# A state-space scan rewritten for sub-chunks of four steps, in a three-block model on one core

## The reference

```python
mag = jnp.exp(lam_re * dt); ang = lam_im * dt          # transition lambda = mag * e^(i ang)
bb_re = q_re[..., None] * br - q_im[..., None] * bi     # q depends on lambda
bu_re = jnp.einsum('blgc,gnc->blgn', u32, bb_re)        # and bu_im
_, _, s_re, s_im = lax.associative_scan(_scan_combine, (a_re_t, a_im_t, bu_re, bu_im), axis=1)
y = (jnp.einsum('blgn,gcn->blgc', s_re, c_re) - jnp.einsum('blgn,gcn->blgc', s_im, c_im) + d_skip * u32)
g = jax.nn.gelu(y); hg = g @ w_glu
out = hg[..., :1024] * jax.nn.sigmoid(hg[..., 1024:])
```

## Time and profile before

| | |
|---|---|
| median of 3 runs | 3033.09 us (3031.11 to 3035.19) |
| profiled execution | 3031.87 us, span 3030.1 us |
| mean granted TensorE clock | 0.99 |
| TensorE, VectorE, ScalarE, GpSimd busy | 97%, 57%, 47%, 2% of the span |
| weights and inputs read | 511.58 MB, 170 GB/s over the span |
| s_in stage, first granule to first of glu | 2468 to 2756 us |

### The profile page before, as it was taken

How to read it: one execution, slowest core, us unless ns; L and a number is a source line. 1 busy time by engine, 2 the same in 40 slices (tenths; PEclk the granted TensorE clock), 3 DMA queues, 4 the chain that set the end, 5 groups by cost and what they waited for, 6 DMA issues and landing times.

```text
span 3030.1 us, 34851 instructions
## 1 busy us (share of the span) xinstructions
PE 2924.2 (97%) x13709; PEld 2403.3 (79%) x13709; DVE 1731.7 (57%) x2222; ACT 1415.6 (47%) x1809; POOL 74.0 (2%) x66
## 2 busy tenths in 40 slices
PE   8999999999999999999999999999999999989998
PEld 7888877788888888878887788888888877556876
DVE  5875655644544454554445545544454569998545
ACT  5543375544444444454446444444444454444444
POOL 0000000000000000000000000000000002210000
PEclk9999999999999999999999999999999999999999
DMA  6532245565555555555552565555655554335443
GB/s 236 176 126 93 89 140 189 179 194 193 181 194 194 194 185 190 193 177 185 188 187 86 175 207 187 190 191 194 194 190 185 194 175 132 98 104 168 172 157 125
DMA packets 255293, 515.45 MB, mean 170 GB/s; under 512 B 8240, under 2 KB 8464, under 8 KB 254144
## 3 DMA queue, kind: packets, MB, share of 16 engines
q1 hardware_dynamic: 252896, 501.61, 50.0%
q0 software_dynamic: 2272, 12.10, 1.2%
HBM read 511.58 MB, written 2.10 MB: 170 GB/s over the span
## 4 chain that ended last, share of the span: by engine, by line
PE 87%; DVE 9%; ACT 2%; issue 2%; DMA 0%; SPq 0%; DVEq 0%; ACTq 0%
PE acc L462 80%; PE side L658 2%; DVE u L1609 2%; DVE u L2210 1%; DVE pc L1609 1%; ACT ar L1009 1%; DVE wlo L1621 1%; DVE ar L1609 1%; PE side L524 1%; PE side L769 1%; PE side L553 1%; DVE ar L1612 0%; ACT whi L1020 0%; DMA raw<-in_ev_w_in 0%; ACT L1009 0%
## 5 line engine op out<-in xcount | busy, mean ns | idle before, releaser
L1621 DVE TENSOR_TENSOR wlo<-raw,whi 128x1024 fp32r<-128x1024 f32 x948 | 1155.3, 1226 | 1114.3 <-ACT whi L1020 1113.5
L1020 ACT ACTIVATE whi<-raw 128x1024 fp32r<-128x1024 f32 x948 | 996.8, 1059 | 1201.3 <-PE acc L462 1199.7
L462 PE MATMUL acc<-whi,xh 128*128 128x512 f32 x3072 | 841.1, 396 | 10.9 <-ACT whi L1020 4.7
L462 PE MATMUL acc<-wlo,xh 128*128 128x512 f32 x3072 | 825.4, 391 | 22.6 <-DVE wlo L1621 22.6
L462 PE MATMUL acc<-whi,xl 128*128 128x512 f32 x3072 | 824.1, 390 | 0.0
L462 PEld LDWEIGHTS acc<-wlo,xh 128*128 128x128 f32 x3072 | 577.6, 188 | 146.7 <-DVE wlo L1621 26.0
L462 PEld LDWEIGHTS acc<-whi,xl 128*128 128x128 f32 x3072 | 578.5, 188 | 122.2
L462 PEld LDWEIGHTS acc<-whi,xh 128*128 128x128 f32 x3072 | 568.9, 189 | 132.7 <-issue 9.6
L462 PE MATMUL acc<-whi,hTh 128*128 128x512 f32 x720 | 194.2, 392 | 2.7 <-ACT u L1009 2.7
L462 PE MATMUL acc<-wlo,hTh 128*128 128x512 f32 x720 | 193.3, 391 | 0.0
L462 PE MATMUL acc<-whi,hTl 128*128 128x512 f32 x720 | 193.3, 390 | 0.0
(11 more groups left out here) (227 smaller groups left out, 1356.5 us busy)
## 6 DMA issues: line engine op xcount, KB each, us to landing
raw<-in_ffn_w_gate SPq DMA_DIRECT2D x88, 1024.0 KB, 5.1
raw<-in_ffn_w_up SPq DMA_DIRECT2D x88, 1024.0 KB, 5.1
raw<-in_ffn_w_down SPq DMA_DIRECT2D x88, 1024.0 KB, 5.0
raw<-in_ev_w_in SPq DMA_DIRECT2D x56, 1024.0 KB, 5.1
raw<-in_od_w_in SPq DMA_DIRECT2D x48, 1024.0 KB, 5.1
raw<-in_w_in SPq DMA_DIRECT2D x32, 1024.0 KB, 5.3
raw<-in_ev_w_out SPq DMA_DIRECT2D x16, 1024.0 KB, 5.0
raw<-in_od_w_out SPq DMA_DIRECT2D x16, 1024.0 KB, 5.0
```

Source lines behind the costliest of these rows:

```text
L462: mm = pe.matmul(acc[2 * pair + t][:], x[:, k0 + j, t * P:t * P + P], w[:, ring, j], start=start and j == 0, stop=stop and j == 1)
L1020: act.activation(whi[:, place % RING], raw_granule(place), ACT.Copy).then_inc(S("hi_done"), 1)
L1621: dve.tensor_tensor(wlo[:, place % RING], raw_granule(place), whi[:, place % RING].bitcast(F32), ALU.subtract).then_inc(S("lo_done"), 1)
```

## The change

The scan works on sub-chunks of four steps (`SUB = 4`). Per group, 4 steps x 16 channels make 64 rows. Four matrices are made from the parameters: `b_lhs` maps the 64 inputs of a sub-chunk to its contribution to the 64 complex states (B times lambda to the power 3 to 0), `c_lhs` maps the state at the end of the sub-chunk before to the 64 outputs (C times lambda to the power 1 to 4), and `t_lhs` maps the inputs to the outputs within a sub-chunk, the skip term included. The recurrence then has 64 steps instead of 256, with lambda to the fourth. Two groups share a 128-partition tile, one on the partitions 0 to 63 and one on 64 to 127, so nearly all its matmuls have 64 rows, 64 weight columns and 64 (or 16) moving columns, in pairs on the two halves (`half(g)`).

What moves or is new, by engine:

- GpSimd: no table arguments any more. The parameters are loaded during the feed-forward layer ahead; 16 transfers of 32 partitions x 512 elements move the projected inputs (`step_pj`) from one place of on-chip memory to another (`xs`), so that sub-chunks lie on partitions. The pooling weights, the last gain row and `p` are loaded later than before.
- TensorE: `turn_b`, `kernel_base`, `kernel_shift`, `turn_u`, `inputs`, `outputs`, `back_steps`, `back_features` in s_in in place of `turn_wide`, `ssm_in`, `ssm_out` and two of four turns; `parameter_columns` and `turn_c` in dn1b.
- VectorE: `angles`, `factors` and `input_matrix` in dn1b; `expand_b` six times, `expand_c` eight times, `table_args` four times, one `rotate` with eight scans of 64 elements and one `unrotate` per channel tile. The gelu result's low part comes from `gate_lo`.
- ScalarE: evacuations of the above, gelu four times on 512 columns instead of eight times on 256, two tables at a time.

The diff, cut to its core:

```diff
-SSM_AT = [22 + 5 * ct for ct in range(8)]
+SUB = 4
+STEPS = TOK // SUB
+V_AT = [17, 23, 28, 34, 39, 43, 47, 51]
+Y_AT = [23, 28, 34, 40, 45, 49, 53, 56]
+BACK_AT = [55, 57, 59, 61]
@@ gpsimd
-            for ct in range(8):
-                pool.tensor_tensor(angle, iota, f, ALU.mult).then_inc(S("tab_arg"), 1)
...
+            for q in range(2):
+                pool.wait_ge(S("projected"), 2 * (PROJ0["s_in"] + q) + 2)
+                for t in range(TT):
+                    for k in range(SUB):
+                        pool.dma_start(xs[64 * q + 32 * t:64 * q + 32 * t + 32, k], step_pj[k:P:SUB, t])\
+                            .then_inc(S("x_moved"), 16)
@@ tensor
+            def turn_c(m):
+                pe.wait_ge(S("bc_in"), 64)
+                b = claim(side[3 - m], "c_turned", m + 1)
+                for ct in range(8):
+                    for g in range(2):
+                        mm = pe.matmul(b[half(g), 64 * ct:64 * ct + 64], c_raw[:, m, ct], pick[:, g],
+                                       start=True, stop=True)
-            def ssm_in(n):
-                for m in range(2):
-                    mm = pe.matmul(b[:, m * TOK:m * TOK + TOK], bt[rows, m, ct], uT[rows, ct], start=True, stop=True)
+            def turn_b(q, f):
+                for r in range(4):
+                    for m in range(2):
+                        for g in range(2):
+                            if g:
+                                mm = pe.matmul(b[half(g), o:o + 64], x, one, start=True, stop=True)
+                            else:
+                                pe.transpose(b[half(g), o:o + 64], x, one)
+            def kernel_base(q):
+                for a in range(16):
+                    for m in range(2):
+                        for g in range(2):
+                            mm = pe.matmul(b[half(g), 16 * a:16 * a + 16], b_exp(q)[half(g), a, m],
+                                           c_bar[half(g), m, 16 * q + a], start=(m == 0), stop=(m == 1))
+            def turn_u(e, bank):
+                pe.wait_ge(S("x_spread"), e + 1)
+                for r in range(8):
+                    mm = pe.transpose(b[:, 64 * r:64 * r + 64], x, ident[half(q), half(q)])
+            def inputs(ct):
+                for r in range(4):
+                    for m in range(2):
+                        for g in range(2):
+                            mm = pe.matmul(b[half(g), o:o + 64], b_lhs[half(g), 4 * ct + r, m], ug[half(g), 4 * ct + r],
+                                           start=True, stop=True)
+            def outputs(ct):
+                for r in range(4):
+                    for g in range(2):
+                        pe.matmul(b[half(g), o:o + 64], t_lhs[half(g), a].rearrange("p t c -> p (t c)"), ug[half(g), a],
+                                  start=True, stop=False)
+                    for m in range(2):
+                        for g in range(2):
+                            mm = pe.matmul(b[half(g), o + 1:o + 64], c_lhs[half(g), a, m], z[half(g), r, m, 0:63],
+                                           start=False, stop=(m == 1))
@@ scalar
+            def x_spread(q):
+                act.wait_ge(S("x_moved"), 128 * (q + 1))
+                for k in range(2):
+                    run(xw[half(q), a], xs.rearrange("p t (a c) -> p a t c", c=16)[half(q), a], ACT.Copy, "x_spread")
@@ vector
+            def expand_b(q, d, n):
+                times_lam(b_bar, d, q)
+                tt(b_exp(q)[:, :, 0, o], by_part(work1)[:, 0], by_part(work2)[:, 1], sub, "expanded")
+                tt(b_exp(q)[:, :, 1, o], by_part(work1)[:, 1], by_part(work2)[:, 0], add, "expanded")
+            def rotate(ct):
+                tt(a, v, cos.unsqueeze(2).to_broadcast([P, 4, 2, STEPS]), mult, "rotated")
+                tt(b[:, :, 0], v[:, :, 1], sin, mult, "rotated")
+                tt(b[:, :, 1], v[:, :, 0], sin, mult, "rotated")
+                tt(z[:, :, 0], a[:, :, 0], b[:, :, 0], add, "rotated")
+                tt(z[:, :, 1], a[:, :, 1], b[:, :, 1], sub, "rotated")
+                for k in range(4):
+                    for m in range(2):
+                        done(dve.tensor_tensor_scan(z[:, k, m], decay, z[:, k, m], 0.0, mult, add))
```

More of the change, by code:

```diff
@@ L539, in features_use, with turn @@
                 return use
-            def turn(name, c):
+            def turn(name, c, halves=(0, 1), bank=None):
                 pe.wait_ge(S("projected"), 2 * (PROJ0[name] + c) + 2)
                 pj = pj_at(name)
-                for j in range(2):
+                for j in halves:
                     n = 2 * TURN[name, c] + j
@@ new lines, in s_aside @@
+                if at_ == 25:
+                    turn_u(3, side[3])
+                if at_ in (26, 28, 30, 32):
+                    turn_b(1, (26, 28, 30, 32).index(at_))
+                if at_ == 27:
+                    kernel_base(1)
+                if at_ == 32:
+                    turn("s_in", 2)
+                if at_ == 35:
+                    b = claim(side[2], "t_done", 5)
+                    kernel_shift(1, 1, b)
+                    kernel_shift(1, 2, b)
+                if at_ == 39:
+                    kernel_shift(1, 3, claim(side[2], "t_done", 6))
@@ new lines, in s_aside @@
+                if at_ == 45:
+                    turn("s_in", 3, (0,), 3)
+                if at_ == 48:
+                    turn("s_in", 3, (1,), 3)
+                for ct in range(8):
+                    if at_ == V_AT[ct]:
+                        inputs(ct)
+                    if at_ == Y_AT[ct]:
+                        outputs(ct)
+                if at_ in BACK_AT:
+                    back_steps(BACK_AT.index(at_))
+                if at_ in (58, 60, 62):
+                    back_features((58, 60, 62).index(at_), side[2])
@@ new lines, in back_out, with gate_hi @@
+            def back_out(e):
+                if e >= 2:
+                    act.wait_ge(S("back2"), e - 1)
+                for k in range(2):
+                    act.wait_ge(S("back1"), 2 * e + k + 1)
+                    q = half(0)
+                    run(at(BACK, 4, CH)[q, 2 * (e % 2) + k].rearrange("p (t a c) -> p a t c", t=SUB, a=8),
+                        side[k][q, :].rearrange("p (a t c) -> p a t c", a=8, t=SUB), ACT.Copy, "back_done")
+            def gate_hi(e, bank):
+                act.wait_ge(S("back2"), e + 1)
+                run(gate_h[:, 2 * e:2 * e + 2].rearrange("p k (j t) -> p k t j", t=SUB),
+                    bank[:].rearrange("p (k t j) -> p k t j", k=2, t=SUB), ACT.Copy, "gh_done")
@@ new lines, in s_aside @@
+                if at_ == 41:
+                    t_out(1, 3, side[2])
+                if at_ == 42:
+                    tables(3)
+                if at_ in (47, 50):
+                    k = (47, 50).index(at_)
+                    act.wait_ge(S("turned"), 2 * TURN["s_in", 3] + k + 1)
+                    run(turned_to("s_in", 3, k), side[3][:].rearrange("p (a b) -> p a b", a=2), ACT.Copy, "turn_done")
+                if at_ in (31, 43, 52, 59):
+                    gelu((31, 43, 52, 59).index(at_))
@@ L2336, in glu_out @@
                            at(SGS, TT, 1024)[:, t, CH * m:CH * m + CH], ALU.mult, "mixed")
[L2338 to L2342 removed]
             def glu_aside(c, j):
+                if (c, j) == (0, 0):
+                    gate_lo(2, side[2])
+                if (c, j) == (0, 1):
+                    gate_lo(3, side[3])
                 for k, where in enumerate(POOL_AT):
```

831 lines of the change are left out of this document (477 added, 354 removed).

## The result

The change makes the kernel faster: 3014.19 us in the median of four runs (3012.33 to 3014.44) against 3034.08 (3031.11 to 3035.19), a ratio of 0.9937, 95% interval 0.9925 to 0.9948. That is 20 us less; forecast were 39 us less. The time lies inside the range of 2970 to 3024, but nearly on the value of a rival (3016) whose mechanism did not happen: that it came near is luck. The profiled execution took 3012.33 us, with a span of 3010.6 us.

What follows compares the result with a forecast made beforehand. VectorE was taken to bound s_in; after, TensorE needs 174.1 + 2.7 start + 60 small work + 8 waits = 245 us against 288, 43 less; the down projection adds 4.2, net 38.8, giving 2994 us, range 2970 to 3024.

Steps and rivals of the forecast that it cites:

- The bound: In s_in: VectorE, busy 263 of 288 us, bounds the stage before; at 187 us after, it stops being the bound.
- The fear for granules 3 to 6: In s_in: weight splits might come late there, where three expansions come while VectorE has just caught up; no size given.
- Overlap of the halves: TensorE's small matmuls on the array's lower and upper 64 rows run at once: 0.027 us a record instead of 0.054.
- serial rival: In s_in: halves run one after the other, small work 81 us in place of 60; 3016 us, chance 0.24.
- dear records: Rival: 64-column weight loads cost 0.10 to 0.11 us without overlap; 3080 us, decided at 0.070 a record, chance 0.09.
- Then the pairs halve: 64 x 0.107: Turning B in s_in: 64 pairs, each of one record and two, cost 0.107 us a pair if the halves overlap.
- a turn and a matmul alternate there: Warning sign for turn_b in s_in: gaps before each turn would make the forecast wrong; no size given.
- I count nothing for it: Clock in s_in, mean 0.96 in stalls before: its loss should go with VectorE's lateness, counted as nothing.
- 60 us of small work: TensorE's small matmuls in s_in, with entering and leaving, lie between 53 and 81 us; 60 was taken.
- full overlap: Small work in s_in if all pairs run at once: 43 us plus 10 for visits; with waits of 1 us, 2979.
- hedge of 7 towards the serial case: Small work in s_in was taken as 60 us, between 53 with overlapping halves and 81 one by one.
- The transfers: Sixteen GpSimd moves of projected inputs in s_in: eight need 10 to 20 us, covered but at their dearest with little slack.

Runs made afterwards that it cites:

- all matmul: The changed kernel with the lower half's transposes in turn_b replaced by matmuls by the identity, so both halves use matmuls; 2985.16 us, ratio 0.9841.
- base split: The all matmul kernel with each kernel_base of 128 records cut into two parts of 64 with granules between; 2982.1 us, ratio 0.9831.
- same half: The changed kernel with turn_b doing the lower half first, alternating transpose and matmul, then eight matmuls on the upper half; 2998.2 us, ratio 0.9884.
- grouped: The changed kernel with turn_b's loops exchanged: eight transposes of the lower half, then the matmuls of the upper half; 2990.5 us, ratio 0.9857.

## Why the prediction was right in part, and where it failed

- **The bound.** Right. Cutting VectorE's scans gives 32 us before and nothing after. Its sum was 170 us, not 187. The fear for granules 3 to 6 did not come true: VectorE is nearly full there (23.2 of 25 us from 2472), but TensorE waits for it once, for 0.3 us.
- **Overlap of the halves.** Right, and in one bank: 32 records of `inputs` in 1.08 us, 0.03 each with entry and exit, against 1.82 us when the halves are kept apart. The serial rival, whose 3016 is close to the time, is refuted by this, and the dear records (0.070 and more) too. The rows of L904, which the forecast read as "as long as four", prove less than it says: the 0.24 us for leaving was itself worked out from four records. What remains is that twelve records of 0.215 us, 2.6 us one by one, took 1.09. The Trainium skill's page TensorEngine Tiling (Array Packing), Restrictions and Gotchas, says that different row tiles cannot access one PSUM bank at the same time. For two 64x64 tiles on the diagonal, which also differ in output partitions, the measurement goes against it.
- **The step that failed** is in "Then the pairs halve: 64 x 0.107". A pair in `turn_b` is a transpose and a matmul, and these neither overlap nor follow closely: 0.43 us a pair at full clock, 27.4 us where the forecast had 6.8. I took the price from rows in which one kind ran alone. That "a turn and a matmul alternate there" stood among the warnings, without a price in the sum or the range. Taking the alternation away gives 29 us; the order alone gives 24.
- **A second term that failed** is the clock, "I count nothing for it". I had expected its loss to go with VectorE's lateness; it cost 14.4 us in the change, nearly all of it around turns of B. The clock falls towards its 1.2 GHz level during the first double turn and again in the second, and once more around granules 30 to 32, where turns of B stand two granules apart (7.28 us for two granules at 2611.01 in place of 5.67). By the chain some 5.2 us of it are small work that ran slowly (slow pairs 3.5, one `kernel_base` 0.9, a turn of the pool input 0.8), and 9.2 us are granules: 4.89, 7.91 and 10.98 us for one, two and three, against 2.95, 5.67 and 8.40, and the two pieces of two between 2611 and 2630.
- **How the 29 us divide.** Without the alternation the turns cost 19.1 us less: 14.3 for the changes of kind (27.4 - 13.1, from the order alone) and 4.8 for the overlap of the halves (13.1 - 8.3). The clock costs 14.4 - 4.7 = 9.7 us less, as all matmul loses 4.7 at its two `kernel_base`.
- **Why the two don't run together.** The change of kind as such was shown; its mechanism was not. The Trainium skill's page TensorEngine Tiling (Array Packing) has two sentences that fit: under Key Properties, that changing the tiling mode drains TensorE, and under Gotcha 2, that column tiling and the transpose mode for FP32 exclude each other on this chip. If these are at work here, every pair changes the mode twice; the 0.17 and 0.26 us from one start to the next do not speak against it, but the page gives no figure and the trace shows no mode.
- **The other terms, and luck.** The forecast had 60 us of small work, 8 of waits and 2.7 for the start, 63.9 without its 6.8 for turns of B. The rest of 223.6 less 174.1 for the granules is 49.5 us. That is 14 too much in the forecast: its own full overlap (43 + 10, less 6.8, and 2.7) gives 48.9, and the hedge of 7 towards the serial case and the 8 us of waits were not needed. So s_in missed by 20.6 us: 20.6 for turns and 14.4 for the clock too little, 14.4 for the rest too much. That the last two cancel is luck, and all matmul lies 9 us below the forecast because of the same 14, less its 4.7 of clock and 1.5 of turns. The last down projection passes s_in on 4.07 us later (first turn of its features 2468.80 against 2464.73), forecast 4.2. The transfers were covered.
- **Open**: by what mechanism a change of kind costs its time, and why the clock falls behind one run of 128 small records and not behind another.

## What to carry to other kernels

Price small TensorE work by the sequence, not by the instruction: look in the order of issue for neighbours of different kind (transpose beside full-precision matmul), and keep kinds together or use one for all. Alternate 64-row matmuls between the two halves, and put full-size matmuls between long runs of tiny ones: behind runs of 128 the clock often fell here and the next large work paid. A warning that a trace cannot price needs a bound in the sum: one change a pair at the 0.24 us that the trace showed for leaving small work would have been 64 x 0.24 = 15 us.

## What the runs showed of the hardware, unexpectedly

- A transpose (fp32, 64x64) beside a matmul of the same shape never starts close behind it: 0.17 us from the transpose's start to the matmul's, 0.26 us from there to the next transpose, whether on the same half or the other. Eight transposes in a row take 0.56 us, 16 matmul records in a row on one half 1.07 us (0.067 each), on alternating halves 0.03 each.
- In all matmul the granted clock fell during or right behind 128 records of 16 columns in a row, with TensorE "busy" all the time (7.31 us for the next two granules). It did not behind 64 in base split (2.95 for the next one); in same half 128 did not lower it at either `kernel_base` (3.84 us, then 5.67 for two granules and 2.95 for one). It fell as well while pairs alternated: in the change a pair goes from 0.43 to 0.64 us at 2499. The Trainium skill's page TensorE: Matmul & The Clock Gate, Part 4, says that a transpose does not count as busy in the same way; the grouped kernel, with as many transposes, kept 1.00 from 2496 to 2506, so no run here shows that the transposes themselves are the cause.
